# The gated-delta mixer rebuilt: row lengths kept as columns, decays made transposed, chunk steps placed between and inside the projection tiles, two chunks inverted in turn

## The chip, the cores and the metric

One core of one Trainium2 chip. The metric is the device time of one execution in microseconds (us); less is better. All arithmetic is fp32, or fp32 split into two fp32r parts (a high part and the remainder) in the large projections.

## The reference, cut to what matters

A block with differential, latent and memory attention and a mixture of experts is followed by a two-layer block. Its first layer's mixer is the part that changes:

```python
def gated_deltanet_mixer(h, w_in, conv_w, a_log, dt_bias, norm_g):
    proj = h @ w_in                              # q, k, v, z, b, a, mem_q
    qkv = jax.nn.silu(causal_depthwise_conv(proj[..., :o1], conv_w))
    q = l2_normalize(...); k = l2_normalize(...)  # 6 heads of 128
    beta = jax.nn.sigmoid(b_logit)
    g = -jnp.exp(a_log) * jax.nn.softplus(a_logit + dt_bias)
    o = gated_delta_rule_chunked(q, k, v, g, beta)
    o = rms_norm(o, norm_g) * jax.nn.silu(z)
```

The rule is S_t = S_{t-1} a_t (I - b_t k_t k_t^T) + b_t v_t k_t^T, o_t = S_t q_t. It is solved by chunks: a unit lower triangular matrix L = strict(b k k^T decay) per head and chunk is inverted and applied to v and k, and a 128 x 128 state per head passes from chunk to chunk. The mixer's output, together with four heads of attention over a memory of 256 rows, goes through w_out. There are 512 tokens and a width of 1024. The kernels use four chunks of 128 tokens.

## The kernel before, in words

Activations are kept with features on partitions and tokens along the row. A projection (class Linear) runs over weight tiles of 128 output columns. SP loads a tile into a ring of six, ScalarE makes its high part (split_high, L230), VectorE the low part (split_low, L236), two tiles ahead, and TensorE makes 8 x 3 products of 512 columns into one of two banks (ps_lin, L275 to L277). Each engine runs a list of stages, fl, in order. A Linear may be given `beside`: stages that each engine runs behind tile j.

The order around the change is: the end of the experts; combine (tokens' sums, transposes back, L1863); gdnin, 26 tiles for q, k, v (6 each, with a convolution of four taps on VectorE at L1964 to L1966 and SiLU on ScalarE), z (6) and the memory queries (2), and beside them the q/k norm (HeadNorm: squares, sums L935, spreads L958); ba, two tiles of six columns for the b and a logits; gates (L2002 to L2032) with heads on six partitions; transposes of v and k to rows (L665); gcb, the cumulated decays spread over partitions (L2065); attention over the memory (mem0: scores L763, turns L776, values L790); gdn_tensor, gdn_scalar, gdn_vector and gdn_gpsimd, which go through the four chunks one after the other; HeadNorm gdn; a split; out0.

In a chunk the inverse is built by doubling: T (the inverse) and R (its transpose) start at blocks of two, and at each of the levels 1 to 6 there are the products U = CM^T T (CM is L masked for the level by GpSimd, L2288), T - R^T U (TU, not at the last level) and R - U^T R (UR), for six heads in two halves of three. ScalarE copies U (L2213), VectorE subtracts (L2260, L2264). Around the levels VectorE makes the decays (L2230 to L2240), L (L2237), the masks (L2245 to L2250) and scaled rows (L2253 to L2255), and TensorE the transposes of L and of the inner products (L2158, L2164).

After the experts GpSimd also scales the residual X by the last norm of the first block (L1834, L1835), while the first gdnin tiles run.

## Time and profile before

| | |
|---|---|
| median of 3 runs | 2389.3 us (2389.22 to 2391.84) |
| profiled execution | 2394.3 us, span 2392.2 us |
| TensorE busy | 2090.8 us, 87% |
| VectorE / ScalarE / GpSimd busy | 1204.6 / 773.6 / 113.6 us |
| granted TensorE clock, mean | 0.911 of 2.4 GHz |

The profile is of one execution. An engine's busy time counts its instructions and not its waits; a row of a timeline gives the start, the duration and, in brackets, the idle time before it and what ended it. An fp32 product shows as two records, a transpose as one. The granted clock has two levels, 2.4 GHz (1.00) and 1.2 GHz (0.50).

### The profile page before, as it was taken

How to read it: one execution, taken by the hardware profiler on the slowest of the kernel's cores; microseconds unless marked ns; L12 is line 12 of the kernel's file. 1: busy time of each engine (PE TensorE's matmuls, PEld its weight loads, DVE VectorE, ACT ScalarE, POOL GpSimd, SP SyncE). 2: the span in 40 equal slices, each digit the busy share in tenths (PEclk: the TensorE clock that was granted, in tenths of full speed). 3: DMA queues.
4: the chain of work that ended last, by engine and by line, in shares of the span. 5: the costliest groups of instructions: out<-in, count | busy, mean ns of one | idle time of the engine just before them, and what ended most of it. 6: DMA issues, size and time to landing. Idle time of an engine off the chain costs nothing.

```text
span 2392.2 us, 25794 instructions
## 1 busy us (share of the span) xinstructions
PE 2090.8 (87%) x10154; PEld 1574.2 (66%) x10154; DVE 1204.6 (50%) x1910; ACT 773.6 (32%) x1498; POOL 113.6 (5%) x81
## 2 busy tenths in 40 slices
PE   6967777886987767998887899999999889999997
PEld 5723444765654436674687678888887668888886
...
DMA packets 77384, 261.08 MB, mean 109 GB/s; under 512 B 9265, under 2 KB 11569, under 8 KB 76753
## 3 DMA queue, kind: packets, MB, share of 16 engines
...
## 4 chain that ended last, share of the span: by engine, by line
PE 73%; DVE 13%; DMA 7%; ACT 4%; issue 2%; SPq 0%; ACTq 0%; DVEq 0%; POOL 0%; POOLq 0%
PE ps_pair L275 17%; PE ps_pair L276 17%; PE ps_pair L277 17%; DMA split_acts_as_f<-w_experts 6%; PE ps_pair L763 3%; PE ps_pair L1602 3%; PE ps_out L790 2%; PE ps_pair L2136 2%; PE ps_turn L776 2%; PE ps_shared L790 2%; PE ps_turn L2136 1%; DVE columns L866 1%; PE ps_out L2136 1%; PE ps_shared L935 1%; PE ps_turn L665 1%
## 5 line engine op out<-in xcount | busy, mean ns | idle before, releaser
L275 PE MATMUL ps_pair<-split_acts,w_high 128*128 128x512 f32 (+1 forms) x1840 | 722.4, 393 | 39.0 <-DVE split_acts L566 20.4
L276 PE MATMUL ps_pair<-split_acts,w_high 128*128 128x512 f32 (+1 forms) x1840 | 715.4, 389 | 0.0
L277 PE MATMUL ps_pair<-split_acts,w_low 128*128 128x512 f32 (+1 forms) x1840 | 715.3, 389 | 0.0
L275 PEld LDWEIGHTS ps_pair<-split_acts,w_high 128*128 128x128 f32 x1840 | 347.3, 189 | 133.5 <-DVE w_low L236 31.3
L236 DVE TENSOR_TENSOR w_low<-w_raw,w_high 128x1024 fp32r<-128x1024 f32 (+6 forms) x259 | 293.0, 1131 | 281.5 <-ACT w_high L230 280.3
L277 PEld LDWEIGHTS ps_pair<-split_acts,w_low 128*128 128x128 f32 x1840 | 346.7, 188 | 74.5
L276 PEld LDWEIGHTS ps_pair<-split_acts,w_high 128*128 128x128 f32 x1840 | 347.4, 189 | 71.7 <-issue 0.2
L230 ACT ACTIVATE w_high<-w_raw 128x1024 fp32r<-128x1024 f32 (+6 forms) x259 | 251.1, 971 | 261.3 <-PE ps_pair L277 226.4
L1602 PE MATMUL ps_pair<-split_acts_as_f 128*64 128x256 f32 x512 | 131.6, 416 | 37.4 <-DMA split_acts_as_f<-w_experts 34.3
L1604 PE MATMUL ps_pair<-split_acts_as_f 128*64 128x256 f32 x512 | 132.0, 417 | 0.0
L345 DVE TENSOR_TENSOR x<-x,ps_pair 128x512 f32<-128x512 f32 x80 | 55.0, 687 | 136.2 <-PE ps_pair L277 136.2
L1602 PEld LDWEIGHTS ps_pair<-split_acts_as_f 128*64 128x64 f32 x512 | 74.1, 150 | 74.7 <-issue 47.3
L776 PE MATMUL ps_turn<-consts,g 128*128 128x128 f32 x320 | 61.8, 333 | 47.3 <-DVE g L887 33.1
L1776 DVE TENSOR_TENSOR g<-g,ps_pair 64x256 f32<-64x256 f32 x31 | 13.2, 425 | 172.8 <-ACT g L1716 172.7
L776 PEld LDWEIGHTS ps_turn<-consts,g 128*128 128x128 f32 x320 | 43.0, 166 | 85.6 <-DVE g L887 49.6
L816 ACT ACTIVATE g<-ps_pair,columns 128x256 f32<-128x256 f32 (+3 forms) x176 | 86.5, 503 | 35.5 <-DVE columns L873 35.5
L763 PE MATMUL ps_pair<-g 64*128 64x256 f32 (+5 forms) x288 | 83.0, 547 | 15.9 <-ACT g L816 10.7
L2318 ACT ACTIVATE split_acts<-h 128x512 fp32r<-128x512 f32 x44 | 27.9, 633 | 192.4 <-DVE h L2331 192.4
L866 DVE TENSOR_REDUCE columns<-ps_pair 128x2 f32<-128x256 f32 (+2 forms) x72 | 69.0, 958 | 30.6 <-PE ps_pair L763 28.5
L1604 PEld LDWEIGHTS ps_pair<-split_acts_as_f 128*64 128x64 f32 x512 | 74.1, 150 | 0.0
L831 ACT COPY split_acts_as_f<-ps_turn 128x512 f32<-128x512 f32 (+3 forms) x112 | 52.5, 498 | 64.2 <-PE ps_turn L776 63.7
L2313 ACT ACTIVATE h<-h 128x512 f32<-128x512 f32 x44 | 27.8, 632 | 134.8 <-DVE h L2324 134.8
...
## 6 DMA issues: line engine op xcount, KB each, us to landing
...
```

What stands on the lines that cost most here:

```text
L230: act.activation(WH[:, t % SPLIT, 0:kt * m], WRAW[:, t % RING, 0:kt * m], ACT.Copy).then_inc(high_ready, 1)
L236: dve.tensor_tensor(WL[:, t % SPLIT, 0:kt * m], WRAW[:, t % RING, 0:kt * m], WH[:, t % SPLIT, 0:kt * m].bitcast(F32), ALU.subtract).then_i ...
L275: pe.matmul(out, wh[:, k, :], self.high(k), start=(k == 0), stop=False)
L276: pe.matmul(out, wh[:, k, :], self.low(k), start=False, stop=False)
L277: last = pe.matmul(out, wl[:, k, :], self.high(k), start=False, stop=(k == self.kt - 1))
L763: last = pe.matmul(self.member(self.bank(m), j, w), lhs, rhs, start=True, stop=True, skip_group_check=True)
L776: last = pe.transpose(ps_t[u % 2][:, at_ * P:(at_ + 1) * P], src, ident)
L790: last = pe.matmul((ps_o, ps_m)[o % 2][rows, q0:q1], lhs, self.turned[h % len(self.turned)][:, slot, src:src + q1 - q0], start=first, stop ...
L866: step(dve, dve.tensor_reduce(top, s, AX_X, ALU.max), "att_dve")
L1602: pe.matmul(out[rows, 0:256], xs, w[:, at_:at_ + 256], start=(k == 0), stop=(k == KT - 1), skip_group_check=True)
L1604: last = pe.matmul(out[high_rows, 0:256], xs, w[:, at_ + 256:at_ + 512], start=(k == 0), stop=(k == KT - 1), skip_group_check=True)
L2136: last = pe.matmul(out, lhs(h), rhs(h), start=True, stop=more is None)
```

## The change

The same function is computed in another order and layout:

- gdnin's tiles come in the order memory queries, k, v, q, z (GDN_ORDER). The ba stage is gone: its 12 columns (WBA, scaled by VectorE) are multiplied by X during combine, with tokens on partitions, eight products of 12 columns per token tile.
- Gates, cumulated decays, and the norms of q and k are columns: tokens on partitions, 24 numbers (4 chunks x 6 heads) per row. q and k are not normalized themselves; their rows are transposed once to sum squares (key_norm, query_norm), and the lengths are multiplied into L, into the inner products, into the scaled rows, and for q into the epsilon of the output norm.
- Decays are made transposed on TensorE (decay: the gates times a triangle of ones), so L^T comes without a transpose (products). T is no longer kept by a product: at each level the root R is transposed (turned_root), so a level is U, R, T: two products and one transpose instead of three products.
- A Linear has `middle` beside `beside`: stages that are issued behind half of a tile's products. Memory attention, gates, decays of chunks 0 and 1, the norms, and the whole inversion of chunk 0 stand beside and in the gdnin tiles. Behind the tiles chunks 1 and 2 are inverted in turn, with the state steps of chunk 0, the rows of 2 and 3 and SiLU of z between them; then chunk 3, with the state steps of chunks 1 and 2 between its levels.
- The state enters as right-hand side (rhs = v - decay k S, then one solve) instead of through w. Outputs have tokens on partitions; their norm is a column per head, and they are transposed back once (gated). Three quarters of out0's input are split before the last chunk ends (feed_early).

In what follows a line that is only "..." stands for lines left out.

```diff
+GDN_ORDER = (24, 25, *range(6, 18), *range(6), *range(18, 24))
...
-          ("gdnin", 26, KT, P, S), ("ba", 2, KT, GDN_HEADS, S), ("out0", KT, KT, P, S)]
+          ("gdnin", 26, KT, P, S), ("out0", KT, KT, P, S)]
...
+                    if k == self.kt // 2 - 1:
+                        for stage in self.middle.get(j, ()):
+                            stage.tensor(pe)
...
+        def ba_tensor(pe, i):
+            need(pe, "comb_act", ("x", i, 1))
+            need(pe, "comb_dve", "wba")
+            for k in range(KT):
+                last = pe.matmul(BA[:, i, :], X[:, k, i * P:(i + 1) * P], WBA[:, :, k, :], start=(k == 0),
+                                 stop=(k == KT - 1))
+            last.then_inc(ba_done, 1)
...
+            pe.matmul(ps_m[:, 0:24], INCT, GATE, start=True, stop=True)
+            done(pe.matmul(ps_m[:, 32:56], const("ones"), GATE, start=True, stop=True), "gate_pe", "sums")
...
+        def decay(c, banks, free):
+            def tensor(pe):
+                need(pe, "gate_dve", "incl")
+                for q in range(2):
+                    need(pe, *free(q))
+                    three(pe, banks[q], q, lambda h: col_of(GATE, c, h).to_broadcast([P, P]), lambda h: INCT, ("e", c, q))
+            def vector(dve):
+                for q in range(2):
+                    need(dve, "c_pe", ("e", c, q))
+                    if c == 2:
+                        dve.wait_ge(tile_done, GDNIN_DONE)
+                    elif c == 3:
+                        need(dve, "c_pe", ("tr", 0, q))
+                    need(dve, "gate_dve", "gc")
+                    three_scaled(dve, q, lambda h: INT[c][:, h, :], lambda n, h: pair(banks[q])[:, n, :],
+                                 lambda h: col_of(GC, c, h), lambda n, h: const("prev"), ALU.subtract, ALU.add,
+                                 ("e", c, q))
+            def scalar(act):
+                for q in range(2):
+                    need(act, "c_dve", ("e", c, q))
+                    h0, h1 = halves[q]
+                    done(act.activation(INT[c][:, h0:h1, :], INT[c][:, h0:h1, :], ACT.Exp), "c_act", ("e", c, q))
+            return On(tensor=tensor, vector=vector, scalar=scalar)
...
+        def products(c, free):
+            banks = chain_banks[c]
+            def tensor(pe):
+                for q in range(2):
+                    need(pe, *free(q))
+                    if q == 0 and c == 0:
+                        need(pe, "conv_act", FIRST_K + GDN_HEADS - 1)
+                    three(pe, banks[q], q, lambda h: kT(h, c), lambda h: kT(h, c), ("kk", c, q))
+            def vector(dve):
+                if c == 1:
+                    dve.wait_ge(tile_done, GDNIN_DONE)
+                elif c:
+                    need(dve, "c_pool", ("C", end_of[c], LEVELS - 1))
+                else:
+                    need(dve, *att_mem0.last)
+                need(dve, "c_dve", "mm")
+                for q in range(2):
+                    need(dve, "c_pe", ("kk", c, q))
+                    need(dve, "c_act", ("e", c, q))
+                    three_scaled(dve, q, lambda h: LT[c][:, h, :], lambda n, h: pair(banks[q])[:, n, :],
+                                 lambda h: col_of(MM, c, h), lambda n, h: INT[c][:, h, :], ALU.mult, ALU.mult,
+                                 ("LT", c, q))
+                need(dve, "c_dve", ("LT", c, 1))
+                if c == 3:
+                    need(dve, "c_pe", ("x", 0, 1))
+                step(dve, dve.scalar_tensor_tensor(out=RR[c], in0=LT[c], scalar=-1.0, in1=wide(level(0)), op0=ALU.mult,
+                                                   op1=ALU.mult), "c_dve")
+                step(dve, dve.tensor_tensor(RR[c], RR[c], wide(ident), ALU.add), "c_dve", ("R", c, 0, 0))
+                ev.seen["c_dve", ("R", c, 0, 1)] = ev.seen["c_dve", ("R", c, 0, 0)]
+            def gpsimd(pool):
+                need(pool, "c_dve", ("R", c, 0, 0))
+                masked(pool, c, 1)
+                pool.tensor_tensor(INT[c], INT[c], wide(ident), ALU.add).then_inc(diagonal_added, 1)
+            return On(tensor=tensor, vector=vector, gpsimd=gpsimd)
...
+        def turned_root(c, l):
+            banks = chain_banks[c]
+            def tensor(pe):
+                for q in range(2):
+                    need(pe, "c_dve", ("R", c, l, q))
+                    three_turned(pe, banks[q], q, lambda h: RR[c][:, h, :], ("T", c, l, q))
+            def scalar(act):
+                for q in range(2):
+                    h0, h1 = halves[q]
+                    need(act, "c_pe", ("T", c, l, q))
+                    if l == 0 and c == 0:
+                        need(act, *att_mem0.last)
+                    done(act.copy(TT[c][:, h0:h1, :], pair(banks[q])), "c_act", ("T", c, l, q))
+            return On(tensor=tensor, scalar=scalar)
+        def step_u(c, l):
+            banks = chain_banks[c]
+            def tensor(pe):
+                need(pe, "c_pool", ("C", c, l))
+                for q in range(2):
+                    need(pe, "c_act", ("T", c, l - 1, q))
+                    three(pe, banks[q], q, lambda h: CM[c][:, h, :], lambda h: TT[c][:, h, :], ("U", c, l, q))
+            def scalar(act):
+                for q in range(2):
+                    h0, h1 = halves[q]
+                    need(act, "c_pe", ("U", c, l, q))
+                    done(act.copy(UU[c][:, h0:h1, :], pair(banks[q])), "c_act", ("U", c, l, q))
+            def gpsimd(pool):
+                if l < LEVELS - 1:
+                    masked(pool, c, l + 1)
+            return On(tensor=tensor, scalar=scalar, gpsimd=gpsimd)
+        def step_r(c, l):
+            banks = chain_banks[c]
+            def tensor(pe):
+                for q in range(2):
+                    need(pe, "c_act", ("U", c, l, q))
+                    three(pe, banks[q], q, lambda h: UU[c][:, h, :], lambda h: RR[c][:, h, :], ("UR", c, l, q))
+            def vector(dve):
+                for q in range(2):
+                    h0, h1 = halves[q]
+                    need(dve, "c_pe", ("UR", c, l, q))
+                    done(dve.tensor_tensor(RR[c][:, h0:h1, :], RR[c][:, h0:h1, :], pair(banks[q]), ALU.subtract), "c_dve",
+                         ("R", c, l, q))
+            return On(tensor=tensor, vector=vector)
...
+        def inner(c, banks, free):
+            def tensor(pe):
+                for q in range(2):
+                    need(pe, *free(q))
+                    if c == 0:
+                        need(pe, "conv_act", FIRST_Q + GDN_HEADS - 1)
+                    three(pe, banks[q], q, lambda h: kT(h, c), lambda h: qT(h, c), ("kq", c, q))
+            def vector(dve):
+                dve.wait_ge(diagonal_added, c + 1)
+                for q in range(2):
+                    need(dve, "c_pe", ("kq", c, q))
+                    three_scaled(dve, q, lambda h: INT[c][:, h, :], lambda n, h: pair(banks[q])[:, n, :],
+                                 lambda h: col_of(MM, c, h), lambda n, h: INT[c][:, h, :], ALU.mult, ALU.mult,
+                                 ("kq", c, q))
+            return On(tensor=tensor, vector=vector)
...
+        def from_state(c):
+            def tensor(pe):
+                for q in range(2):
+                    need(pe, *(("c_act", ("S", 0, q)) if c == 1 else ("c_dve", ("S", c - 1, q))))
+                    three(pe, state_banks[q], q, lambda h: kT(h, c), lambda h: ST[:, h, :], ("kS", c, q))
...
+        def next_state(c):
+            def tensor(pe):
+                for q in range(2):
+                    need(pe, "c_act", ("x", c, q))
+                    need(pe, "c_dve", ("KG", c, q))
+                    three(pe, state_banks[q], q, lambda h: KG[c][:, h, :], lambda h: VR[c][:, h, :], ("kv", c, q))
...
+        beside, middle = defaultdict(list), defaultdict(list)
+        chunk_steps = []
+        def at_tile(j, *stages):
+            beside[j] += stages
+            chunk_steps.extend(stages)
+        def in_tile(j, *stages):
+            middle[j] += stages
+            chunk_steps.extend(stages)
+        gate_read = lambda q: ("gate_dve", "ngam")
+        mem0_out = lambda o: ("att_act", ("out", att_mem0.o0 + o))
+        key_squared = lambda h: ("norm_act", ("k", "square", h))
+        query_squared = lambda h: ("norm_act", ("q", "square", h))
+        at_tile(0, mix0_roots, On(scalar=gates_scalar, vector=gates_vector))
+        at_tile(1, On(tensor=sums_tensor, scalar=sums_scalar, vector=sums_vector))
+        at_tile(2, decay(0, state_banks, gate_read), att_mem0.scored(0))
+        at_tile(3, decay(1, state_banks, lambda q: ("c_dve", ("e", 0, q))), att_mem0.weighed(0))
+        at_tile(4, att_mem0.turned_over(0), att_mem0.scored(1))
+        at_tile(5, key_norm(0, ps_m, ("c_dve", ("e", 1, 1))),
+                On(tensor=lambda pe: need(pe, "c_dve", ("e", 1, 0))), att_mem0.summed(0), att_mem0.weighed(1))
+        at_tile(6, key_norm(1, ps_m, key_squared(0)), att_mem0.turned_over(1), att_mem0.scored(2))
+        at_tile(7, key_norm(2, ps_m, key_squared(1)), att_mem0.summed(1), att_mem0.weighed(2))
+        at_tile(8, key_norm(3, ps_m, key_squared(2)), att_mem0.turned_over(2), att_mem0.scored(3))
+        at_tile(9, key_norm(4, ps_o, mem0_out(0)), On(tensor=lambda pe: need(pe, *key_squared(3))),
+                att_mem0.summed(2), att_mem0.weighed(3))
+        at_tile(10, key_norm(5, ps_o, key_squared(4)), att_mem0.turned_over(3))
+        at_tile(11, att_mem0.summed(3), On(scalar=key_roots_scalar, vector=key_roots_vector))
+        last_turn = ("turn_act", turns["n"] - 1)
+        at_tile(12, products(0, lambda q: last_turn))
+        at_tile(13, turned_root(0, 0))
+        in_tile(14, step_u(0, 1))
+        at_tile(14, step_r(0, 1))
+        in_tile(15, turned_root(0, 1))
+        at_tile(15, step_u(0, 2))
+        in_tile(16, step_r(0, 2))
+        at_tile(16, turned_root(0, 2))
+        in_tile(17, step_u(0, 3))
+        at_tile(17, query_norm(0, ps_o, key_squared(5)), step_r(0, 3))
+        in_tile(18, turned_root(0, 3))
+        at_tile(18, On(tensor=lambda pe: need(pe, *mem0_out(1))), query_norm(1, ps_m, query_squared(0)), step_u(0, 4))
+        in_tile(19, step_r(0, 4))
+        at_tile(19, query_norm(2, ps_o, query_squared(1)), turned_root(0, 4))
+        in_tile(20, step_u(0, 5))
+        at_tile(20, query_norm(3, ps_m, query_squared(2)), step_r(0, 5))
+        in_tile(21, turned_root(0, 5))
+        at_tile(21, query_norm(4, ps_o, query_squared(3)), step_u(0, 6))
+        in_tile(22, step_r(0, 6))
+        at_tile(22, query_norm(5, ps_m, query_squared(4)), rows_in(0, "KG", ps_s, lambda q: att_mem0.last))
+        in_tile(23, rows_in(0, "VR", ps_s, lambda q: ("c_dve", ("KG", 0, q))))
+        at_tile(23, inner(0, ps_s, lambda q: ("c_dve", ("VR", 0, q))), On(vector=query_roots_vector))
+        for j in range(FIRST_K, FIRST_Z):
+            beside[j].append(convolve(j))
+        fl.append(Linear("gdnin", hi, lo, n_mix0.ready, gdn_act, gdn_dve, beside=beside, middle=middle))
+        def lin_read(q):
+            return "c_dve", ("z", 0, q)
+        def gdnin_read(pe):
+            wait_stage_evac(pe, "gdnin")
+        both = (1, 2)
+        steps = [On(tensor=gdnin_read), decay(2, ps_lin, lambda q: ("c_dve", ("kq", 0, q))),
+                 products(1, lambda q: ("c_dve", ("kq", 0, q))), products(2, lambda q: ("c_dve", ("R", 0, LEVELS - 1, q))),
+                 solved(0), rows_in(1, "KG", ps_lin, lambda q: ("c_dve", ("e", 2, q))), turned_root(1, 0),
+                 rows_in(1, "VR", ps_lin, lambda q: ("c_dve", ("KG", 1, q))), turned_root(2, 0), next_state(0),
+                 gate_silu(0), gate_silu(1)]
+        between = {
+            (1, "r"): [rows_in(2, "KG", ps_lin, lambda q: ("c_dve", ("VR", 1, q))), gate_silu(2), gate_silu(3)],
+            (1, "t"): [rows_in(2, "VR", ps_lin, lambda q: ("c_dve", ("KG", 2, q))), gate_silu(4), gate_silu(5)],
+            (2, "u"): [inner(1, ps_lin, lambda q: ("c_dve", ("VR", 2, q)))],
+            (2, "t"): [inner(2, ps_lin, lambda q: ("c_dve", ("kq", 1, q)))],
+            (3, "u"): [outputs(0, lambda q: ("c_dve", ("kq", 2, q)))],
+            (3, "r"): [normed(0)],
+            (4, "u"): [gated(0)],
+            (4, "t"): [decay(3, ps_lin, lin_read)],
+            (5, "u"): [rows_in(3, "KG", ps_lin, lambda q: ("c_dve", ("e", 3, q)))],
+            (5, "t"): [rows_in(3, "VR", ps_lin, lambda q: ("c_dve", ("KG", 3, q)))],
+            (6, "u"): [from_state(1)],
+        }
+        for l in range(1, LEVELS):
+            for kind, made in (("u", step_u), ("r", step_r), ("t", turned_root)):
+                if l < LEVELS - 1 or kind != "t":
+                    steps += [made(c, l) for c in both]
+                    steps += between.get((l, kind), [])
+        lin_free = lambda c: lambda q: (("c_dve", ("VR", 3, 0)) if q == 0 else ("c_dve", ("kq", 3, 0))) if c == 1 else \
+            ("c_dve", ("z", c - 1, q))
+        other_free = lambda c: lambda q: (("c_dve", ("VR", 3, 1)) if q == 0 else ("c_dve", ("kq", 3, 1))) if c == 1 else \
+            ("c_dve", ("o", c - 1, q))
+        u, r, t = step_u, step_r, turned_root
+        steps += [products(3, lambda q: ("c_dve", ("R", 2, LEVELS - 1, q))), solved(1),
+                  inner(3, ps_s, lambda q: ("c_dve", ("R", 1, LEVELS - 1, q))), read_state(1, lin_free(1)), t(3, 0),
+                  next_state(1), outputs(1, other_free(1)), u(3, 1), from_state(2), r(3, 1), normed(1), t(3, 1), solved(2),
+                  u(3, 2), gated(1), r(3, 2), read_state(2, lin_free(2)), t(3, 2), next_state(2), u(3, 3),
+                  outputs(2, other_free(2)), r(3, 3), from_state(3), t(3, 3), normed(2), u(3, 4), gated(2),
+                  r(3, 4), read_state(3, lin_free(3)), t(3, 4), feed_early(6, 8), u(3, 5), feed_early(0, 2), r(3, 5), feed_early(2, 4), t(3, 5),
+                  feed_early(4, 6), u(3, 6), r(3, 6), solved(3), outputs(3, other_free(3)), normed(3), gated(3), feed_late(0),
+                  feed_late(1)]
```

## Rows read from the trace of the kernel before

**Rows 1.** page, part 4: share of the chain that ended last, by engine

```profile
PE 73%; DVE 13%; DMA 7%; ACT 4%; issue 2%; SPq 0%; ACTq 0%; DVEq 0%; POOL 0%; POOLq 0%
```

**Rows 2.** windows: length, busy us (instructions) by engine, TensorE clock, DMA share, GB/s

```profile
917.00:1102.00 185.00, 184.70 (x736) 128.97 (x737) 124.55 (x156) 59.49 (x82) 25.77 (x16) 0.98 0.23 75
1102.00:1163.50 61.50, 49.49 (x149) 29.34 (x149) 18.64 (x47) 29.77 (x74) 0.00 (x0) 0.61 0.00 1
1163.50:1353.50 190.00, 160.75 (x1248) 153.37 (x1248) 125.00 (x200) 48.53 (x97) 49.41 (x25) 0.90 0.00 1
1353.50:1377.50 24.00, 16.36 (x24) 3.73 (x24) 12.72 (x15) 6.70 (x11) 0.47 (x1) 0.71 0.04 11
```

**Rows 3.** timeline, TensorE: start, us taken, line, operation, count [idle before]

```profile
912.79 1.97 PE L1863 MATMUL ps_turn<-consts,g 128*128 128x128 f32 x8 [2.87 <-DVE g L1898]
917.16 0.77 PE L275 MATMUL ps_pair<-split_acts,w_high 128*128 128x512 f32 x1 [2.40 <-DVE split_acts L566]
...
925.60 1.05 PE L1915 MATMUL ps_shared<-consts,roots 128*128 128x128 f32 x8
...
927.30 0.48 PE L275 MATMUL ps_pair<-split_acts,w_high 128*128 128x512 f32 x1
...
932.86 0.39 PE L275 MATMUL ps_pair<-split_acts,w_high 128*128 128x512 f32 x1
...
944.79 0.50 PE L275 MATMUL ps_pair<-split_acts,w_high 128*128 128x512 f32 x1
...
951.43 0.50 PE L275 MATMUL ps_pair<-split_acts,w_high 128*128 128x512 f32 x1
```

**Rows 4.** timeline, VectorE: the split of a tile's weights, four times

```profile
933.45 1.60 DVE L236 TENSOR_TENSOR w_low<-w_raw,w_high 128x1024 fp32r<-128x1024 f32 x1
...
940.10 1.60 DVE L236 TENSOR_TENSOR w_low<-w_raw,w_high 128x1024 fp32r<-128x1024 f32 x1
...
958.53 1.23 DVE L236 TENSOR_TENSOR w_low<-w_raw,w_high 128x1024 fp32r<-128x1024 f32 x1
...
963.27 1.23 DVE L236 TENSOR_TENSOR w_low<-w_raw,w_high 128x1024 fp32r<-128x1024 f32 x1
```

**Rows 5.** timeline, ScalarE: a table load and the activation behind it

```profile
1102.65 1.28 ACT L2027 ACT_TABLE_LOAD   x1 [5.19 <-DVE g L1996]
1103.95 0.20 ACT L2027 ACTIVATE columns<-vectors 6x1 f32<-6x1 f32 x1
```

**Rows 6.** timeline of the second chunk, all engines

```profile
1214.26 1.64 DVE L2237 SCALAR_TENSOR_TENSOR split_acts_as_f<-ps_pair,columns,h 128x128 f32<-128x128 f32 x6
...
1218.98 2.45 DVE L2246 TENSOR_TENSOR split_acts_as_f<-consts,split_acts_as_f 128x768 f32<-128x768 f32 x1
...
1222.45 0.96 DVE L2250 TENSOR_TENSOR split_acts_as_f<-consts,split_acts_as_f 128x768 f32<-128x768 f32 x1
...
1230.27 1.81 POOL L2288 TENSOR_TENSOR h<-split_acts_as_f,consts 128x768 f32<-128x768 f32 x1 [3.20 <-PE ps_pair L2136]
...
1232.87 1.50 PE L2136 MATMUL ps_pair<-split_acts_as_f,h 128*128 128x128 f32 x12
1233.07 0.56 DVE L2264 TENSOR_TENSOR split_acts_as_f<-split_acts_as_f,ps_shared 128x384 f32<-128x384 f32 x1
1233.74 0.48 ACT L2213 COPY split_acts_as_f<-ps_pair 128x384 f32<-128x384 f32 x1 [3.04 <-PE ps_pair L2136]
...
1237.06 1.50 PE L2136 MATMUL ps_pair<-split_acts_as_f,h 128*128 128x128 f32 x12
```

**Rows 7.** windows (columns as in rows 2)

```profile
1110.00:1120.00 10.00, 8.66 (x36) 6.43 (x34) 2.40 (x6) 4.55 (x11) 0.00 (x0) 0.50 0.00 0
...
1210.00:1220.00 10.00, 4.84 (x34) 4.01 (x32) 8.81 (x18) 2.59 (x6) 1.90 (x1) 0.84 0.00 0
1900.00:1920.00 20.00, 19.56 (x125) 15.68 (x124) 18.91 (x48) 14.18 (x51) 0.00 (x0) 1.00 0.01 1
```

**Rows 8.** groups of instructions, TensorE, 1900 to 1920: busy us, mean ns, idle before

```profile
L776 PE MATMUL ps_turn<-consts,g 128*128 128x128 f32 x32 | 4.4, 280 | 0.4 <-DVE g L891 0.4
```

685 lines of the change are left out of this document (377 added, 308 removed).

## The prediction

> **What bounds the kernel now.** I read the page first: TensorE holds 73% of the chain of waits [rows 1]. The changed code lies in one stretch, so I asked for the windows of its stages [rows 2]. The projection tiles run from 917 to 1102 with TensorE busy 184.7 of 185.0 us at clock 0.98. Then come three stages that TensorE does not fill: 61.5 us for logits, gates, row transposes and memory attention (clock 0.61), 190.0 us for the four chunks (0.90, busy 161 us), 24.0 us for the head norm. The first tile starts at 917.16 [rows 3] and out0 at 1377.5 [rows 2]: 460.3 us. The forecast is the new length of this stretch; the rest keeps its time.
>
> TensorE's timeline gives the unit prices. A tile takes 932.86 - 927.30 = 5.56 us. With a guest of two 512-column records behind it the period is 951.43 - 944.79 = 6.64 [rows 3], 1.08 more; by columns (below) the records are 0.93 of that, and as a place in the middle of a tile breaks the stream twice I charge 0.24 to each guest for entry and exit. In a chunk a level is 36 records in 1237.06 - 1232.87 = 4.19 us, 0.116 each [rows 6]. An fp32 product of 128 columns is two records, so "six" (two halves of three products) are 1.39 us; a transpose is one record, six are 0.70. Within levels TensorE is full already. A chunk's 312 records x 0.116 = 36.2 us of some 47.5 (190.0 / 4): it loses 11.3 us around its levels, where VectorE prepares masks and decays and the clock falls.
>
> **The change part by part.**
>
> *Removed:* both ba tiles (11.1), the q/k norm's twelve sums and spreads, the serial stage of gates and transposes, the TU product of each level, the w products, the head norm stage. *Added:* everything below. As order and waits are new, I build the stretch anew.
>
> *Combine.* The ba products of token tiles 2 and 3 stand behind the last transposes (912.79 to 914.8 [rows 3]) and ahead of tile 0: 32 records at 0.23 (twice 0.116, for the low clock), 7.5 us, to 922.3. Before, tile 0 took 925.60 - 917.16 = 8.44, 2.9 over a tile, so its first 5.8 us were at the low clock. Now TensorE is dense from 912.8, and tile 0 should run at the higher: 5.56, to 927.6 (bounds: 926 and 931). The two small loads on SP's queue precede expert pieces whose first are loaded already: nothing, bound 1 us.
>
> *Tiles.* 25 more tiles: 139.0. Guests: roots 1.7 [rows 3]; sums 0.5; two decays 2.8; four score groups (8 records of 256 columns, by columns 1.86 each) 7.4; four turns 3.7; four value groups 7.4; twelve norms of four transposes 5.6; products and inner 2.8; six U and six R, 16.7; six turned roots 4.2; KG and VR 1.4. Together 54.2. They stand in 34 places (24 behind a tile, 10 in the middle of one), x 0.24 = 8.2. The gates' chain to the sums holds two table loads of 1.28 [rows 5] and some ten small operations; TensorE waits 1.3 for it behind tile 1.
>
> Does another engine bind? VectorE's cycle for a convolution tile, split to split, is 963.27 - 958.53 = 4.74 alone and 940.10 - 933.45 = 6.65 while GpSimd works [rows 4]. At tiles 2 and 3 decay (1.64 for six scaled products [rows 6]) and softmax bring some 9.9, against 9.0 and 7.1 on TensorE: a lag of 4 us, within the two tiles that splits run ahead. At tiles 14 to 19, 6.65 + 1.2 for R = 7.8 against 5.56 + 0.48 + 2.1 = 8.1. So the masks' contention is just hidden; without that cover each tile pays its excess. ScalarE at tiles 6 and 8: split 1.05, SiLU 0.63, squares 1.4, turns 1.1, exponentials 1.8 (estimates by columns from its other rows), two loads 2.56: 8.5 against 9.1. The tiles end at 927.6 + 139.0 + 54.2 + 8.2 + 1.3 = 1130.3.
>
> On the loads: ScalarE computes 1103.95 - 1102.65 = 1.30 after a load starts [rows 5], so a load costs 1.3 in this kernel. The Trainium skill (ScalarE: Activation LUTs, What ACT_TABLE_LOAD costs) adds a drain of 1.38 us to each. With the page's price tiles 4, 6 and 8 would be ScalarE's by some 2 us each and the sum up to 6 higher; the trace does not show the drain.
>
> *Entry to the pair.* TensorE waits 0.95 for the last take. It runs decay 2, products 1 and 2, solved 0, KG and VR of chunk 1, two turned roots, next state: 5 x 1.39 + 4 x 0.70 = 9.7. VectorE needs 1.64 for the decay, twice 1.64 + 0.96 + 0.96 for the products, then KG, and its second pair meets GpSimd's first mask, where 0.96 became 2.45 [rows 6]. KG ends 12.7 after the tiles do, and VR on TensorE needs its bank: 5 idle. Such a gap lowers the clock for a while [rows 7]: 2. Together 17.7 (bounds 10.7 and 25), to 1148.0.
>
> *Pair.* Six levels of U, U, R, R, T, T less the last T: 24 x 1.39 + 10 x 0.70 = 40.3. Between them, five sixes of products (7.0) and five of transposes (3.5). GpSimd has two masks of 1.81 to 2.5 a level against 6.95: hidden. ScalarE copies (0.48 each [rows 6]) eight times; at level 3 the outputs' squares and the load for the square root delay T by 2; 1 elsewhere. 53.8, to 1201.8.
>
> *Tail.* 27 sixes of products and 9 of transposes: 43.8. I walked through it with 0.2 from a product to its reader, 0.05 back, 0.5 per ScalarE half and 0.6 per VectorE half [rows 6]. Two long waits: read_state(1)'s second half shares a bank with inner(3), which VectorE may take only when GpSimd has masked (1.8) and added the diagonal (1.8) after chunk 3's R at 4.7, so TensorE stands 4.7 there; and behind the last R come solve, copy, product, add, squares, mean, root, reciprocal, scale, transpose, gate and split, 8 beyond their products. Single levels add 4. The walk ends at 60.3; for the clock I take 5 more (bounds 0 and 35). 65.3, to 1267.1.
>
> New length 1267.1 - 917.2 = 349.9, a gain of 110.4. The profiled execution took 2394.3, so 2283.9 for it; the median of the runs is 5.0 below it, so **2278.9**.
>
> **Rivals.**
>
> *Everything hidden.* VectorE and GpSimd run ahead and only the end's 8 remain: entry 10.7, pair 50.8, tail 51.8, gates 0. The sum falls by 7.0 + 3.0 + 13.5 + 1.3 = 24.8: **2254**. For it: within levels TensorE is full [rows 6]. Against: the bank waits that I name.
>
> *Queues and clock.* Each of 34 guests waits 0.3 more (10), and the tail's single chain leaves gaps that keep the clock low: its 43.8 become 87.6, with the 8 beyond 95.6, 30.3 more. **2319**. For it: in 1210 to 1220, with gaps, the clock sank to 0.84, in the logits stage to 0.61 [rows 2, 7]; against: in 1900 to 1920, at 19.6 of 20 us busy with softmax steps in turn, it stayed at 1.00 [rows 7].
>
> *Transposes do not hold the clock.* Row transposes, 8.7 of 10 us busy, ran at 0.50 [rows 7], and the change puts transposes for products into every level. If they kept the whole stretch behind the tiles low (9.7 + 50.8 + 43.8 = 104.3, of which 7 are charged), the time would be **2376**. Against: 32 transposes among the 125 records of 1900 to 1920, at 1.00 [rows 7, 8]. The Trainium skill (TensorE: Matmul & The Clock Gate, Part 4: PE-mode transpose) says that transposes do not count as busy for the clock; for a stretch of transposes alone the trace agrees (0.50).
>
> *Slower.* The clock falls among the tiles because guests interrupt them, in the middle too. At half the clock 139.0 + 54.2 = 193 us are added: **2472**. It turns the sign once 110.4 / 193 = 57% of that stretch is low. Against: the tiles before had 25 guests and 0.98 [rows 2].
>
> **How the numbers follow.** Forecast 0.57 (its own range 2262 to 2300), all hidden 0.12, queues and clock 0.23, transposes 0.04, slower 0.04. Faster by over 0.2% (4.8 us, about what a measurement of this kernel can tell from no change) are the first three and most of the fourth, with a little off for partial clock loss: 0.94. Within it 0.02, slower 0.04. The range 2252 to 2320 leaves out both clock cases and the far ends of the others.
>
> **What the profile would show.** Right: tiles end near 1130 at clock 0.95 or more; a slot of U or R costs 1.6; a level of the pair takes 6.9 to 7.5; TensorE waits once for some 5 us at the entry, released by VectorE's KG, and once in the tail before the second half of the product of q and state; out0 starts near 1267. Wrong: TensorE in the tiles waiting for w_low or a take; the clock at 0.5 through the tail; many waits of over 1 us for ScalarE; or a change outside the stretch.

## The result and the profile after

The changed kernel takes 2268.6 us (median of 4 runs, 2267.4 to 2274.1) where the one before took 2390.1 on the same chip: a ratio of 0.949, 95% interval 0.948 to 0.951, 121.5 us less. Forecast were 2278.9 and a gain of 110.4. The profiled execution took 2267.4, its span is 2265.5.

Four stages are named in what follows: the tiles of gdnin (until 1121.1 us), the entry to the pair, the pair (chunks 1 and 2 inverted in turn, from 1138.4) and the tail (chunk 3, from 1188.8 to out0). Their windows (columns as in [rows 2]: length, then TensorE, its weight loads, VectorE, ScalarE and GpSimd busy, clock, DMA):

```profile
918.40:1121.30 202.90, 199.69 (x1013) 162.83 (x1013) 141.06 (x220) 98.28 (x241) 39.02 (x23) 0.99 0.21 68
1121.30:1138.40 17.10, 11.40 (x84) 10.89 (x85) 13.02 (x27) 4.28 (x9) 7.87 (x4) 0.90 0.01 1
1138.40:1188.80 50.40, 49.31 (x440) 48.77 (x438) 25.49 (x63) 30.22 (x73) 17.93 (x10) 1.00 0.00 1
1188.80:1251.00 62.20, 49.87 (x381) 46.84 (x381) 36.19 (x88) 31.02 (x98) 13.98 (x8) 0.91 0.02 5
```

Against [rows 2]: in place of 61.5 us at clock 0.61, 190.0 at 0.90 and 24.0 at 0.71 there are 129.0 us (1121.1 to out0 at 1250.13) at 0.90, 1.00 and 0.91; the tiles took up the rest of the work at 0.99 and ended 19 us later. Nothing outside moved: from out0's first product to the end of the span 1014.7 us before, 1015.4 after. From gdnin's first product to out0's first it is 331.7 us in place of 460.3, 128.6 less; the medians differ by 7 less than this, for a reason given with the sum below.

A guest is work of a chunk or of the attention that stands beside or in a tile. TensorE's timeline around two guests of chunk 0, its first U and its R, and then the first records of tiles 16 and 17:

```profile
1033.24 1.58 PE L2139 MATMUL ps_turn<-split_acts_as_f 128*128 128x128 f32 x12 [2.65 <-ACT split_acts_as_f L2286]
...
1037.41 1.50 PE L2139 MATMUL ps_turn<-split_acts_as_f 128*128 128x128 f32 x12
1038.66 0.48 PE L276 MATMUL ps_pair<-split_acts,w_high 128*128 128x512 f32 x1
...
1046.14 0.48 PE L276 MATMUL ps_pair<-split_acts,w_high 128*128 128x512 f32 x1
...
1053.61 0.47 PE L276 MATMUL ps_pair<-split_acts,w_high 128*128 128x512 f32 x1
```

From the start of R (1037.41) to the next record of the tile it is 1.25 us. This is not yet its price, since the records of the tile behind a guest stand wider apart at first. The price is in the period: tile 16, with one R and one turned root (18 records) as guests, takes 1053.61 - 1046.14 = 7.47, and 5.44 where it has no guest (in e6, below). The bracket on 1033.24, in tile 14, is the only wait of over 0.6 us in all of the tiles.

The waits of TensorE of 1 us and more in the stretch, by what they wait for (us in total, times, longest); all waits of over 0.3 us add up to 21.9:

```profile
PE ps_pair L2144 <- DVE split_acts_as_f L2367: 4.9, 1, 4.9
PE ps_pair L2139 <- DVE h L2149: 4.3, 1, 4.3
PE ps_turn L2139 <- ACT split_acts_as_f L2286: 4.1, 4, 2.7
PE ps_pair L2144 <- DVE h L2496: 2.8, 1, 2.8
PE ps_turn L2144 <- DVE split_acts_as_f L2321: 2.4, 2, 2.2
PE ps_pair L276 <- DVE split_acts L2541: 1.3, 1, 1.3
```

The entry, TensorE: the gap before VR of chunk 1, the transposes of v to rows. KG are those of k, ahead of it.

```profile
1128.28 0.88 PE L2144 MATMUL ps_pair<-consts,split_acts_as_f 128*128 128x128 f32 x6
1134.05 1.37 PE L2144 MATMUL ps_pair<-consts,g 128*128 128x128 f32 x6 [4.90 <-DVE split_acts_as_f L2367]
...
1138.42 1.50 PE L2139 MATMUL ps_pair<-split_acts_as_f 128*128 128x128 f32 x12
```

VectorE's timeline in that gap:

```profile
1128.26 1.64 DVE L2149 SCALAR_TENSOR_TENSOR split_acts_as_f<-ps_turn,g,split_acts_as_f 128x128 f32<-128x128 f32 x6
1129.93 1.00 DVE L2253 SCALAR_TENSOR_TENSOR split_acts_as_f<-split_acts_as_f,consts 128x768 f32<-128x768 f32 x1
1130.96 2.44 DVE L2255 TENSOR_TENSOR split_acts_as_f<-split_acts_as_f,consts 128x768 f32<-128x768 f32 x1
1133.44 1.02 DVE L2367 TENSOR_TENSOR split_acts_as_f<-ps_pair,g 128x384 f32<-128x384 f32 x2
```

GpSimd's (chunk 1's mask, then its diagonal):

```profile
1128.30 1.82 POOL L2270 TENSOR_TENSOR split_acts_as_f<-split_acts_as_f,consts 128x768 f32<-128x768 f32 x1 [43.91 <-DVE split_acts_as_f L2255]
1130.07 2.51 POOL L2261 TENSOR_TENSOR h<-h,consts 128x768 f32<-128x768 f32 x1
```

VR waits for the bank of KG. VectorE, in order, first finishes chunk 2's L (1128.26) and its root. The root's last operation takes 2.44 us beside GpSimd's diagonal, where [rows 6] shows 0.96 alone. VectorE takes KG at 1133.44.

The tail: the second half of q times state, the R of level 5, the first transposes of gated(3), out0.

```profile
1192.96 0.83 PE L2139 MATMUL ps_pair<-scratch,g 128*128 128x128 f32 x6
1198.14 0.94 PE L2139 MATMUL ps_pair<-scratch,g 128*128 128x128 f32 x6 [4.35 <-DVE h L2149]
...
1235.71 1.01 PE L2144 MATMUL ps_turn<-consts,split_acts_as_f 128*128 128x128 f32 x6 [2.23 <-DVE split_acts_as_f L2321]
...
1247.21 1.58 PE L2144 MATMUL ps_pair<-consts,h 128*128 128x128 f32 x6 [2.77 <-DVE h L2496]
1250.13 0.77 PE L276 MATMUL ps_pair<-split_acts,w_high 128*128 128x512 f32 x1 [1.34 <-DVE split_acts L2541]
```

### The profile page after: what moved, and what is told of

It is laid out like the page before. It is cut to its first block, busy times and chain, and to the rows that moved or that the text cites. A ratio compares the mean times of both kernels' runs of the same rounds, so it can differ in the third digit from the quotient of the medians.

```text
span 2265.5 us, 25512 instructions
## 1 busy us (share of the span) xinstructions
PE 2001.4 (88%) x9978; PEld 1541.7 (68%) x9978; DVE 1138.6 (50%) x1894; ACT 793.7 (35%) x1655; POOL 118.8 (5%) x85
## 4 chain that ended last, share of the span: by engine, by line
PE 73%; DVE 12%; DMA 8%; ACT 4%; issue 2%; POOL 0%; SPq 0%; ACTq 0%; DVEq 0%; POOLq 0%
PE ps_pair L276 17%; PE ps_pair L278 17%; PE ps_pair L277 17%; DMA split_acts_as_f<-w_experts 6%; PE ps_pair L792 3%; PE ps_pair L1631 3%; PE ps_turn L2139 2%; PE ps_out L819 2%; PE ps_shared L819 2%; PE ps_turn L805 2%; DVE columns L895 1%; PE ps_pair L2139 1%; DMA w_raw<-w_mem 1%; DVE ps_pair L885 1%; DVE g L920 1%
## 5 line engine op out<-in xcount | busy, mean ns | idle before, releaser
L237 DVE TENSOR_TENSOR w_low<-w_raw,w_high 128x1024 fp32r<-128x1024 f32 (+5 forms) x257 | 291.8, 1136 | 291.4 <-ACT w_high L231 289.6
L231 ACT ACTIVATE w_high<-w_raw 128x1024 fp32r<-128x1024 f32 (+5 forms) x257 | 251.1, 978 | 235.3 <-PE ps_pair L278 201.9
L805 PE MATMUL ps_turn<-consts,g 128*128 128x128 f32 x320 | 61.5, 331 | 47.2 <-DVE g L916 33.1
```

The lines of the kernel that those rows point to most:

```text
L231: act.activation(WH[:, t % SPLIT, 0:kt * m], WRAW[:, t % RING, 0:kt * m], ACT.Copy).then_inc(high_ready, 1)
L237: dve.tensor_tensor(WL[:, t % SPLIT, 0:kt * m], WRAW[:, t % RING, 0:kt * m], WH[:, t % SPLIT, 0:kt * m].bitcast(F32), ALU.subtract).then_i ...
L805: last = pe.transpose(ps_t[u % 2][:, at_ * P:(at_ + 1) * P], src, ident)
```

## The experiments

All are edits of the changed kernel; each ratio is to the kernel before, timed beside it. "Stretch" is measured in each trace from gdnin's first product to out0's first (1250.13 - 918.40 = 331.7 in the changed kernel: 202.7 of tiles and 129.0 behind them). It is free of what scatters elsewhere, where medians of 4 or 5 runs still scatter by some 2 us. It has a scatter of its own, by the clock alone. In tile 0, which no edit but e11 touches, 6 to 10 records ran at the low clock, 0.2 us each. Behind tile 14's wait of 2.65 to 2.67 the clock fell in two traces (e2 and e5; the tile takes 12.67 there) and not in those of the changed kernel, e1 and e10 (11.05 to 11.09). So a difference of under 2 us between two stretches means little unless the timeline shows where it lies. Only the cuts of the diffs that matter are shown; in them a line that is only "..." stands for lines left out.

**e1_state.** Is the bank behind the wait of 4.35?

```diff
-inner(3, ...), read_state(1, lin_free(1)), t(3, 0), next_state(1), outputs(1, ...)
+inner(3, ...), t(3, 0), next_state(1), read_state(1, lin_free(1)), outputs(1, ...)
```

> Only the order of three steps behind solved(1) changes: the transpose of chunk 3's root and next_state(1) go ahead of read_state(1). Theory (the bank wait): TensorE stands 4.35 us before the second half of q times state because VectorE can't empty the bank of inner(3) until GpSimd has masked and added the diagonal, and the clock then sinks for some 4 us (1.5 us lost). The moved work (0.65 of transposes, 2.7 of products) is ready and fills the gap: the wait falls under 1.5 us and the time falls by 3 to 5 us, to 2264 to 2266. Rival (the chain of chunk 3 binds): the wait returns before the next step of the state, since the state's update now comes later; no gain, 2268 to 2269.

2265.7 us, ratio 0.947 (0.946 to 0.948); stretch 328.1, 3.7 less. 1.73 of the wait are left, released by the same VectorE product: the moved work filled the rest. The theory holds, with a little more of the wait left than its 1.5; the chain of chunk 3 did not bind.

**e2_entry.** Is it VectorE's order that holds the entry?

```diff
-turned_root(1, 0), rows_in(1, "VR", ...), turned_root(2, 0), next_state(0),
+turned_root(1, 0), next_state(0), step_u(1, 1), step_r(1, 1),
+rows_in(1, "VR", ...), turned_root(2, 0),
```

> At the entry to the pair the first U and R of chunk 1 and next_state(0) go ahead of the transposes of v (VR) of chunk 1. Theory (TensorE stands because VectorE, in order, reaches KG only at 1133.4): the 4.90 us of idle before VR take 4.0 us of work that is ready (two products of chunk 1 and the state), no low clock behind it; 4 to 5.5 us less, 2263 to 2265. Rival (VectorE is the bound of the entry): the subtraction of the moved R, 1.0 us, and KG and VR still end at 1135.5 and later, the transposed root of chunk 1 and U of chunk 2 wait for them, and at most 2 us are won: 2266.5 to 2268.5.

2265.6, ratio 0.947 (0.946 to 0.948). The gap before VR fell from 4.90 to 0.74, but a new wait of 1.54 stands before R of chunk 2, for ScalarE's copy behind the table load and SiLU of z:

```profile
1138.53 1.01 PE L2144 MATMUL ps_pair<-consts,g 128*128 128x128 f32 x6 [0.74 <-DVE split_acts_as_f L2367]
...
1143.65 1.60 PE L2139 MATMUL ps_turn<-split_acts_as_f 128*128 128x128 f32 x12 [1.54 <-ACT split_acts_as_f L2302]
```

The stretch is 330.0. Its tiles took 1.0 longer, which the edit does not touch: 1.6 of low clock behind the wait in tile 14, less 0.7 in tile 0. What stands behind the tiles fell from 129.0 to 126.3. Of 4.9 us of waiting 2.75 were gained: between the two expectations.

**e3_feed_shift** and **e9_conv_first.** What makes tile 14 wait, and level 5?

```diff
-in_tile(14, step_u(0, 1)); at_tile(14, step_r(0, 1)); in_tile(15, turned_root(0, 1)) ...
+at_tile(14, step_u(0, 1)); in_tile(15, step_r(0, 1)); at_tile(15, turned_root(0, 1)) ...
-u(3, 5), feed_early(0, 2), r(3, 5), feed_early(2, 4), t(3, 5), feed_early(4, 6), u(3, 6), r(3, 6)
+u(3, 5), r(3, 5), feed_early(0, 2), t(3, 5), feed_early(2, 4), u(3, 6), r(3, 6), feed_early(4, 6)
```

> Two edits in different places. (1) The steps of chunk 0 from its first U on each stand half a tile later, the last R behind tile 22. (2) The last three early splits of out0's input each stand one product later, so that VectorE subtracts for R first. Theory for 1: the 2.65 us wait in tile 14 is for a copy that ScalarE makes only after the SiLU of a convolution that VectorE finishes late (products, and 5.25 in place of 2.33 us beside GpSimd); half a tile later the copy is there: wait 0, 2.65 us won. Rival for 1: VectorE's lag is real work and the wait moves to a low part or a take in tile 15 or 16. Theory for 2: TensorE's 2.23 us wait for the subtraction in level 5 goes, and 0.9 before it: 2 to 3 us won. Rival for 2: the splits only move the wait to level 6 or behind the last R. Both theories: 4 to 5.5 us less, 2263 to 2265; both rivals: 2267 to 2269.

2266.0, ratio 0.948 (0.946 to 0.949). The second edit took away the wait of 2.23 and the low clock behind it, and the part behind the tiles fell by 3.4. The wait of 0.9 ahead of it, which was also expected to go, stayed at 0.88: it is for ScalarE's copy of the turned root, and not for the splits. The first edit moved the wait by half a tile: 1.77 before R of level 1. e9 keeps only this shift, puts the first turned root into tile 14 and lets VectorE make the convolution of tile 12 ahead of chunk 0's products (the lines of the shift are left out):

```diff
-at_tile(13, turned_root(0, 0))
+in_tile(14, turned_root(0, 0))
-beside[j].append(convolve(j))
+beside[j].insert(0 if j == 12 else len(beside[j]), convolve(j))
```

> The half-tile shift of e3_feed_shift, without its change to the splits; VectorE makes tile 12's convolution before the products of chunk 0, and the first transposed root stands inside tile 14. Theory (the 2.65 us, and the 1.77 that were left of it, are ScalarE's copy behind a SiLU whose convolution waited for the products): no wait over 0.5 us is left in tiles 13 to 16, tile stretch 202.7 to 200.0 to 200.6, time 2.2 to 2.7 less, 2266. Rival (VectorE's load in tiles 12 to 14 is too large in any order): at least 1.2 us of waiting is left somewhere in tiles 13 to 16, tile stretch above 201.3.

2268.5, ratio 0.949 (0.948 to 0.950), tiles 202.0: the rival, in the orders tried. Its VectorE around the wait, and then its ScalarE:

```profile
1024.67 2.33 DVE L2046 SCALAR_TENSOR_TENSOR scratch<-h,vectors,scratch 128x512 f32<-128x512 f32 x3
...
1033.94 5.33 DVE L2046 SCALAR_TENSOR_TENSOR scratch<-h,vectors,scratch 128x512 f32<-128x512 f32 x3
```

ScalarE:

```profile
1039.30 0.63 ACT L2026 ACTIVATE g<-scratch 128x512 f32<-128x512 f32 x1 [5.84 <-DVE scratch L2046]
1039.84 0.84 ACT L2302 COPY split_acts_as_f<-ps_turn 128x384 f32<-128x384 f32 x2
```

Three taps of a convolution take 2.33 us alone and 5.33 beside GpSimd's two operations. ScalarE, in order, makes that tile's SiLU (1039.30) and only then the copy that TensorE waits for (1.61 us). In all three orders that were tried the copy stands behind a convolution that shares with GpSimd.

**e4_together.** The edits of e1, e2 and e3.

> All four edits of the three kernels before. If they are independent their gains add up: 11 to 16 us less than 2268.6, 2253 to 2258. If one wait only stood ahead of another, less than the sum of the three: above 2259.

2256.8, ratio 0.943 (0.942 to 0.944), stretch 320.6: 11.1 less, where the three alone gave 3.7, 1.8 and 4.0 (9.4; 11.0 if the 1.6 of low clock in e2's tile 14, which e4 does not have, is left out). The theory holds: the waits are independent.

**e5_serial.** What is it worth to invert two chunks in turn?

```diff
-for l in range(1, LEVELS):
+for c in both:
+    for l in range(1, LEVELS):
...
-            steps += [made(c, l) for c in both]
-            steps += between.get((l, kind), [])
+                steps.append(made(c, l))
+                if (l <= 3) == (c == 1):
+                    steps += between.get((l, kind), [])
```

> Chunks 1 and 2 are inverted one after the other, not in turn; the steps between the levels are kept, those of levels 1 to 3 in chunk 1, those of 4 to 6 in chunk 2. Theory (the second chunk covers copies and subtractions): TensorE waits 0.5 to 1 us for the copy behind each transposed root, as in the tail (0.89 at level 5), 12 levels: 6 to 12 us more, 2275 to 2281, clock 0.95 or more in the stretch. Rival A (the steps between the levels cover enough): under 3 us more, below 2271.6. Rival B (the gaps bring the clock down): over 20 us more, above 2289.

2279.6, ratio 0.953 (0.952 to 0.955); behind the tiles 140.6 in place of 129.0. Compare a bare level (one with nothing between its steps) of one chunk, from U to U, with the two chunks in turn in the changed kernel, R of level 2 to R of level 3. First e5's TensorE:

```profile
1163.57 3.08 PE L2139 MATMUL ps_pair<-split_acts_as_f 128*128 128x128 f32 x24 [1.83 <-ACT split_acts_as_f L2286]
1166.62 1.22 PE L2144 MATMUL ps_pair<-consts,split_acts_as_f 128*128 128x128 f32 x6
1167.83 3.08 PE L2139 MATMUL ps_pair<-split_acts_as_f 128*128 128x128 f32 x24
```

The changed kernel's:

```profile
1151.40 1.50 PE L2139 MATMUL ps_pair<-split_acts_as_f 128*128 128x128 f32 x12
...
1160.75 1.50 PE L2139 MATMUL ps_pair<-split_acts_as_f 128*128 128x128 f32 x12
```

It is 4.26 us alone. In turn it is 9.35 from R to R with two groups of other products of 1.34 in it, so 3.33 a chunk and no wait. Inverting in turn is worth 0.93 at each bare level, and 11.6 us in all: the theory.

**e6_chunk0_behind.** What do the tiles cover?

```diff
-in_tile(14, step_u(0, 1)) ... in_tile(22, step_r(0, 6))
+steps = [..., products(1, ...), *first, products(2, ...), ...]   # first: levels 1 to 6 of chunk 0
```

> The levels of chunk 0 are taken out of the tiles and stand behind them, ahead of products(2). Theory (guests in the tiles save only the waits between levels): U and R cost 1.34 in place of 1.25 (12 of them, 1.1 us), 0.5 to 0.9 us of waiting at each of six levels, 3 to 5.5, against them the 2.65 us wait in tile 14, which goes: 1 to 4 us more, 2270 to 2273; the tiles shorten from 202.7 to some 181. Rival A (VectorE beside the levels was what held the tiles): the tiles shorten by more than 24 us and the time falls. Rival B (a single chain behind the tiles lets the clock sink): over 10 us more, above 2279.

2271.8, ratio 0.950 (0.949 to 0.951). The tiles shortened by 21.3 to 181.4, and what stands behind them grew by 25.4. Net 4.0 us: in the range of the theory. Rival A, over 24 us off the tiles, is out.

The theory's terms did not all come true. Its first, that a guest in a tile is cheaper than the same records in a row of their own (1.25 against 1.34), does not hold. Here tile 16 has no guest:

```profile
1040.69 0.39 PE L276 MATMUL ps_pair<-split_acts,w_high 128*128 128x512 f32 x1
...
1046.13 0.39 PE L276 MATMUL ps_pair<-split_acts,w_high 128*128 128x512 f32 x1
```

5.44 us against 7.47 with two guests of 18 records: 2.03 for what takes 1.34 + 0.66 = 2.00 in the pair. Tiles 14 to 22 together give the same: 75.0 against 53.6 us, or 19.6 for the levels when the waits in them are taken out (2.65 and 0.77), and 12 x 1.34 + 5 x 0.655 = 19.4 in a row. So the tiles cover the waits between the levels, and only these. A new wait of 3.80 for GpSimd's second mask, behind the mask and diagonal of chunk 1, was not expected. It adds little, since the wait before VR, now behind chunk 0's levels, fell from 4.90 to 1.05.

**e7_turns4.** Do transposes let the clock fall?

```diff
+for _ in range(3 if c else 0):
+    for n, h in enumerate(first_last(q)):
+        pe.transpose(pair(banks[q])[:, n, :], RR[c][:, h, :], ident)
 three_turned(pe, banks[q], q, lambda h: RR[c][:, h, :], ("T", c, l, q))
```

> Every transpose of a root of chunks 1, 2 and 3 is issued four times. Added: 18 x 6 x 3 = 324 transposes at 0.11 us, 35.6 us, of which up to 6 fall into waits. Theory (transposes among products hold the clock): 30 to 36 us more, 2298 to 2305, granted clock 0.98 or more in the pair. Rival (transposes do not count as work for the clock): transposes are then half of TensorE's time in a level, the clock sinks in pair and tail, at half of it for half of the time over 50 us more on top, above 2350.

2298.2, ratio 0.962 (0.960 to 0.963), 29.6 more; the part behind the tiles grew by 31.4. A window in the pair:

```profile
1140.00:1200.00 60.00, 59.28 (x536) 59.09 (x535) 21.34 (x52) 29.08 (x67) 17.93 (x10) 1.00 0.00 1
```

The clock stayed at 1.00 in it, with transposes taking about half of TensorE's time (8 x 0.65 of 10.6 us in a bare level), and 324 of them cost 0.097 each net of the waits that they fill. The rival is out.

**e8_masks_twice.** Is VectorE just hidden in tiles 14 to 19?

```diff
+if c == 0:
+    step(pool, pool.tensor_tensor(CM[c], LT[c], wide(level(l)), ALU.mult), "twice_pool")
 done(pool.tensor_tensor(CM[c], LT[c], wide(level(l)), ALU.mult), "c_pool", ("C", c, l))
```

> GpSimd makes each mask of chunk 0 twice, so that it shares with VectorE for twice as long in tiles 13 to 21; the output is the same. Theory of the prediction (VectorE is just hidden in these tiles, 7.8 us a tile against TensorE's 8.1): each added mask costs VectorE 1.2 to 1.5 us, TensorE 0.9 to 1.2 at each of the last five or six: 5 to 8 us more, 2273.5 to 2276.5. Rival (VectorE has room: it idles 0.9 and 2.7 us in tiles 15 and 16): under 1.5 us more, below 2270.

2273.2, ratio 0.951 (0.950 to 0.952); tiles 205.2, 2.5 longer. All of it lies in tile 14, which takes 14.09 us in place of 11.07:

```profile
1036.16 2.89 PE L2139 MATMUL ps_turn<-split_acts_as_f 128*128 128x128 f32 x12 [4.08 <-ACT split_acts_as_f L2288]
```

The wait grew from 2.65 to 4.08 (the convolution ahead of it from 5.25 to 6.67), and the clock was low behind it (0.79 from 1036 to 1044), 1.6 us, as in e2 and e5 without the added masks. Tile 0 took 0.6 less. Tiles 15 to 23, with the five other masks, have the same periods as before, to 0.01 us. So one tile is bound by this chain, and the others have all the room that the rival gives them; the prediction's "just hidden" is wrong for them. The median rose by 4.6, more than the trace's stretch shows; what the rest is stays open.

**e10_end.** Can the last chain be filled?

```diff
+On(tensor=lambda pe: out0.tensor_early(pe, (6, 7), ("c_act", ("qS", 3, 0)))), gated(3), ...
```

tensor_early issues the six records of out0's first tile for k = 6 and 7; the transposes of gated(3)'s first half go to another bank, and ScalarE takes the root of half 0 ahead of the squares of half 1.

> At the end: the products of out0's first tile with the memory columns (6 records, ready since level 5) stand ahead of the transposes of gated(3); the root of half 0 is taken before the squares of half 1. Theory (the end is a chain of copies and small operations in which TensorE idles 2.77 and 1.34 us): 2.6 us of products at the low clock go into the first gap, out0's last product of tile 0 comes 2 to 3.2 us earlier: 2265.5 to 2266.5. Rival (the clock pays it back: out0 starts at the low clock for as long as before): 1.3 us or less.

2264.2, ratio 0.947 (0.946 to 0.949). From the end of the tiles to the end of out0's second tile the trace gives 139.8 in place of 141.7: 1.9 us, between the two. The median fell by 4.4; the rest of that is not in this stretch. The six records ran at the high clock in the gap (1.4 us), and TensorE's waits from there on fell from 4.11 to 2.84. Behind the gap the clock is low as before: seven of the remaining records last over 0.6 us, eight in the changed kernel.

**e11_ba_late.** Do the ba products cost what they take?

```diff
-ba_tensor(pe, QT - 1)                                   # and ba_tensor(pe, 2), in combine
+at_tile(0, On(tensor=lambda pe: [ba_tensor(pe, i) for i in (QT - 2, QT - 1)]), mix0_roots, ...
```

> The products for b and a of token tiles 2 and 3 (32 records, 6.84 us at the low clock) stand behind gdnin's tile 0, where the clock is high. Theory (the low clock lasts as long from TensorE's restart whatever it does): tile 0 starts some 5 to 6 us earlier but runs all 8 us of it at the low clock, 10.2 us, and the 32 records take 3.6: from the last transposes of combine to tile 1 nothing or up to 1.5 us is won, and the gates' later start gives a wait of 3 us before the sums: 0 to 3 us more, 2268.5 to 2271.5. Rival (the products just cost half there): 3 us less, 2265.6.

2269.9, ratio 0.949 (0.948 to 0.951), which does not tell it from the changed kernel. The 32 records fell from 6.84 to 3.63 us, and yet from the last transposes to tile 1 it took 18.8 us in place of 17.7. The changed kernel's TensorE first:

```profile
909.97 1.95 PE L1918 MATMUL ps_turn<-consts,g 128*128 128x128 f32 x8
911.71 6.84 PE L1903 MATMUL ps_out<-g,x 128*128 128x12 f32 x32
918.40 0.77 PE L276 MATMUL ps_pair<-split_acts,w_high 128*128 128x512 f32 x1
...
927.66 0.48 PE L276 MATMUL ps_pair<-split_acts,w_high 128*128 128x512 f32 x1
```

And e11's:

```profile
913.49 1.97 PE L1918 MATMUL ps_turn<-consts,g 128*128 128x128 f32 x8 [1.00 <-DVE g L1959]
917.86 0.77 PE L276 MATMUL ps_pair<-split_acts,w_high 128*128 128x512 f32 x1 [2.40 <-DVE split_acts L574]
...
925.83 3.63 PE L1903 MATMUL ps_out<-g,x 128*128 128x12 f32 x32
929.32 1.58 PE L1976 MATMUL ps_shared<-consts,roots 128*128 128x128 f32 x8
...
932.26 0.77 PE L276 MATMUL ps_pair<-split_acts,w_high 128*128 128x512 f32 x1
```

Counted from the last transposes, tile 0 starts 4.4 us behind them in place of 8.4. It could not come sooner, since it waits 2.40 for VectorE's low part of the input, a wait that the products fill in their old place. The 4.1 us won are lost again: the products take 3.5 behind tile 0, tile 0 itself 0.4 more, and the clock is low right behind the products (0.59 from 929.32 to 932.26), so that the roots' products take 2.94 where they took 1.70. The second expectation is wrong. The first has the right number by luck: tile 0 did not run at the low clock throughout (11 records, nine in the changed kernel), and the gates' sums did not wait.

**e12_best.** e4, e9 and e10 together, SiLU of z ahead of R of chunk 1, and chunk 3's diagonal ahead of its mask.

> All edits that the runs so far speak for: those of e4_together, of e9_conv_first and e10_end, SiLU of the first two z tiles in ScalarE's idle time ahead of R of chunk 1, and GpSimd adds chunk 3's diagonal before it masks. Theory: 2256.8 less 1.8 (what is left in tile 14), 2.5 (end), 2 (bank wait of 1.7 and the low clock behind it), 1.5 (wait of R behind SiLU): 2247.5 to 2251. Rival (the gains are of the same waits): above 2253.

2255.6, ratio 0.944 (0.942 to 0.945): by the number, the rival. To the end of out0's second tile the stretch is 331.8 us against 333.8 in e4: 2 us less. The medians (2256.8 for e4) can't tell them apart. The wait for SiLU went. The bank wait went too, and stands one step earlier. TensorE:

```profile
1189.24 1.11 PE L2161 MATMUL ps_turn<-consts,split_acts_as_f 128*128 128x128 f32 x6 [1.91 <-DVE split_acts_as_f L2272]
1190.14 1.49 PE L2156 MATMUL ps_out<-split_acts_as_f 128*128 128x128 f32 x6
```

VectorE:

```profile
1186.74 2.44 DVE L2272 TENSOR_TENSOR split_acts_as_f<-split_acts_as_f,consts 128x768 f32<-128x768 f32 x1
```

GpSimd's diagonal now shares with VectorE's second operation on the root (2.44 us for 0.96), and the transpose waits 1.91 for it and brings the low clock with it. At the end 14 records of out0 last 0.6 us or more, ten in e4 and eight in the changed kernel: the low clock takes back 0.8 us against e4.

## Why the prediction was right, and where it was too high

The sign, the size and the places of the long waits were right; the total was 10.3 us too high. The changed kernel's profiled execution took 16.5 less than the 2283.9 that the sum gave for it; 6 of this do not show in the medians, since before's profiled execution lay 4 to 5 above its median and after's 1 below: it is luck that the total looks this near. The stretch itself was to end at 1267.1 and ended at 1250.1, 17.0 sooner. By the steps of the sum:

- **Combine**: tile 0 to end at 927.6 (its terms, 922.3 and 5.56, make 927.9), measured 925.96. The 32 records took 6.84 at the low clock (7.5 forecast), but tile 0 did not run at the higher clock from its start: behind its first, the records up to the tenth stand 0.43 apart, 7.56 for the tile where the sum has 5.56. What hides this is mostly luck: tile 0 started at 918.4 and not at 922, because combine's last transposes started at 909.97, 2.8 sooner than in the trace before (912.79). The experts ahead of them ended 2.6 sooner in this execution (881.6 against 884.1); in the traces of the edits that point lies anywhere from 882.5 to 885.7.
- **Tiles**: 202.7 forecast from tile 0's end, 195.2 measured. This is the largest miss, and it is in a price: what a guest adds to a tile. A tile without guests takes 5.44 (tile 16 of e6). The sum's unit of 5.56 was read right behind a guest and so already held an entry; then 0.24 was charged again for each of 34 places. With waits of 3.2 us taken out, the guests and their places took 195.2 - 25 x 5.44 - 3.2 = 56.0. The sum has 54.2 + 8.2 for them and 3.0 more in its unit, 65.4. At the 1.34 for twelve records that the pair shows, in place of 1.39, the guests alone would be some 52 (an estimate), which leaves about 4 for all entries and exits, 0.1 a place, where 11.2 stood. "A slot of U or R costs 1.6" is wrong in the same way: 1.25 from start to start, and some 1.35 by the period (12 of the 18 records that add 2.03). The waits took 1.9 more than the sum's 1.3.
- **Gates**: 1.3 forecast, 0.52 measured. VectorE "just hidden" was wrong: e8 and e9 show one place, tile 14, where a convolution next to GpSimd's operations holds ScalarE's queue, and TensorE with it for 2.65 us, which I had not foreseen, and room everywhere else.
- **Entry**: 17.7 forecast, 17.3 measured (1121.1 to 1138.42), with the wait of 5 at its place, released by VectorE's KG (4.90).
- **Pair**: 53.8 forecast, 50.4 measured. A level was to take 6.9 to 7.5; a bare one takes 6.66. Waits were to be 3, the ones over 0.3 are 0.72 and 0.38.
- **Tail**: 65.3 forecast, 61.3 measured. The wait before the second half of q times state was 4.35 (4.7 forecast). The end was to be 8 beyond its products, it is 5.5: from the end of R at 1241.3 to 1250.1, less 3.3 of products. The clock took at most 5.6 (0.09 of 62.2, less where TensorE idled anyway), charged were 5. Of the single waits the sum has 4 in all; they measured 3.8, but the largest, 2.23 for a subtraction that stands behind a split on VectorE, was not named.

On the rivals: "everything hidden" is wrong by the waits above. e4 and e12 show what order alone can hide of their 21.9 us: 13.6 are left in e4 and 10.4 in e12. "Queues and clock" is wrong: guests wait only in tile 14 (2.65) and for the gates (0.52), and the tail kept 0.91 of its clock. "Transposes do not hold the clock" is out by e7. What the Trainium skill says (TensorE: Matmul & The Clock Gate, Part 4: PE-mode transpose) agrees with [rows 7] for transposes alone; e7 shows that in the pair, with half of TensorE's time in products, the clock stayed at 1.00. The slower rival is out: 0.99 in the tiles. On table loads the trace stays with its own price: the next activation begins 1.30 us after a load does in tiles and pair, with no drain of 1.38 beside it as the Trainium skill has it (ScalarE: Activation LUTs, What ACT_TABLE_LOAD costs), and TensorE waited for nothing in tiles 4, 6 and 8.

Where the gain came from: e5 puts 11.6 us to the inversion in turn, e6 4.0 us to chunk 0's levels in the tiles rather than behind them; e11 gives 1 us for ba's place. Most of the rest is work that is gone or runs at the high clock: the stages after the tiles had 226.6 us of TensorE busy before [rows 2] and have 110.6 now. Over the whole stretch the windows give 411.3 us busy and 49.2 idle before, 310.3 and 22.3 now. So some 27 us of the gain are idle time and 101 are busy time. Of the busy time at most some 44 are the clock (an estimate: each window's length times what its clock lacks of 1.00 adds up to 54 before and 9 now), and the other 57 or more are work that is gone. How much of that is the turned root in place of a product, and how much the norms by columns, was not tried.
